# Small loads of the beginning on other queues, x in quarters, the first weights split by inner tiles, bias DMAs ahead of the first projection job

## The reference

```python
h = rms_norm(x, norm1_g[l])                                   # x: (1, 256, 1024)
p = jnp.einsum('bsd,de->bse', h, w_in[l])                     # w_in: (1024, 2560)
q, k, v = ...                                                 # 8 heads of 64 each
q = rms_norm(q, q_norm_g[l]); k = rms_norm(k, k_norm_g[l])
bias = rel_bias[:, jnp.clip(dist, -128, 128) + 128]           # (8 heads, 257) spread over distances
p = jax.nn.softmax(jnp.where(valid, q @ k.T * d ** -0.5 + bias, NEG_INF))
```

## Time and profile before

| | us |
|---|---|
| median of three runs | 1808.47 (1807.52 to 1809.2) |
| the profiled execution | 1807.76 |
| its span on the core | 1806.0 |
| PE busy | 1740.0 (96%) |
| DVE busy | 1336.2 (74%) |
| ACT busy | 1161.0 (64%) |
| POOL busy | 63.8 (4%) |

### The profile page before, as it was taken

One profiled execution on the slowest core, in us unless ns is written; L12 is line 12 of the kernel. 1 busy time (PEld: TensorE's weight loads), 2 busy tenths in 40 slices (PEclk: granted clock), 3 DMA queues, 4 the chain that ended last, 5 costly groups with the idle time before them and its releaser, 6 DMA issues.

```text
span 1806.0 us, 23347 instructions
## 1 busy us (share of the span) xinstructions
PE 1740.0 (96%) x8588; PEld 1427.8 (79%) x8588; DVE 1336.2 (74%) x1191; ACT 1161.0 (64%) x1179; POOL 63.8 (4%) x64
## 2 busy tenths in 40 slices
PE   7899999989999989889999999999999999999998
PEld 6677888877788876668888888888888888888886
DVE  5664444676554458568888898898888898888988
ACT  5545543665544358647777777777777776776775
POOL 1010000130000000020000000000000000000000
PEclk9899999999999999979999999999999999999999
DMA  9545553545556454139999989999999999999995
GB/s 340 168 151 177 186 187 123 175 154 163 189 184 192 158 174 129 39 124 360 374 326 371 366 326 365 349 346 367 344 353 370 329 370 364 325 366 348 345 368 224
DMA packets 230600, 481.74 MB, mean 267 GB/s; under 512 B 12020, under 2 KB 55560, under 8 KB 230544
## 3 DMA queue, kind: packets, MB, share of 16 engines
q1 hardware_dynamic: 220224, 470.99, 73.3%
q10 hardware_dynamic: 10320, 9.99, 1.7%
HBM read 479.08 MB, written 2.65 MB: 267 GB/s over the span
## 4 chain that ended last, share of the span: by engine, by line
PE 68%; DVE 5%; ACT 4%; issue 2%; ACTq 0%; DMA 0%; DVEq 0%; POOL 0%
PE bank L631 21%; PE bank L634 20%; PE bank L632 20%; PE bank L1179 2%; ACT w_hi L1744 1%; PE bank L1211 1%; PE bank L1066 1%; DVE x L2286 1%; DVE w_lo L2306 1%; PE bank L625 1%; DVE w_lo L1801 1%; ACT w_hi L1281 1%; ACT L1744 0%; ACT e L1363 0%; ACT dwq L1656 0%
## 5 line engine op out<-in xcount | busy, mean ns | idle before, releaser
L2306 DVE TENSOR_TENSOR w_lo<-raw,w_hi 128x2048 fp32r<-128x2048 f32 x336 | 764.3, 2289 | 118.5 <-ACT w_hi L1744 115.7
L1744 ACT ACTIVATE w_hi<-raw 128x2048 fp32r<-128x2048 f32 x336 | 639.3, 1920 | 173.3 <-PE bank L634 173.2
L1801 DVE TENSOR_TENSOR w_lo<-raw,w_hi 128x2048 fp32r<-128x2048 f32 (+3 forms) x118 | 256.0, 2173 | 150.9 <-ACT w_hi L1281 150.5
L631 PE MATMUL bank<-w_hi,xg_hi 128*128 128x512 f32 x896 | 355.7, 397 | 5.9 <-DVE w_lo L2306 4.4
L634 PE MATMUL bank<-w_hi,xg_lo 128*128 128x512 f32 x896 | 350.5, 391 | 0.0
L632 PE MATMUL bank<-w_lo,xg_hi 128*128 128x512 f32 x896 | 349.9, 391 | 0.0
L631 PE MATMUL bank<-w_hi,a_hi 128*128 128x512 f32 (+3 forms) x672 | 263.1, 391 | 12.5 <-DVE a_lo L2165 4.4
L1281 ACT ACTIVATE w_hi<-raw 128x2048 fp32r<-128x2048 f32 (+3 forms) x118 | 213.1, 1811 | 91.9 <-PE bank L634 85.5
L634 PE MATMUL bank<-w_hi,a_lo 128*128 128x512 f32 (+3 forms) x672 | 256.1, 381 | 0.0
L632 PE MATMUL bank<-w_lo,a_hi 128*128 128x512 f32 (+3 forms) x672 | 256.0, 381 | 0.0
L631 PEld LDWEIGHTS bank<-w_hi,xg_hi 128*128 128x128 f32 x896 | 169.0, 189 | 42.4 <-DVE w_lo L2306 7.3
(11 more groups left out here) (229 smaller groups left out, 1695.3 us busy)
## 6 DMA issues: line engine op xcount, KB each, us to landing
raw<-in_moe_w_gate SPq DMA_DIRECT2D x114, 1024.0 KB, 7.0
raw<-in_moe_w_up SPq DMA_DIRECT2D x113, 1024.0 KB, 7.1
raw<-in_moe_w_down SPq DMA_DIRECT2D x112, 1024.0 KB, 6.5
raw<-in_w_mlp SPq DMA_DIRECT2D x32, 1024.0 KB, 5.2
raw<-in_ffn_w_gate SPq DMA_DIRECT2D x22, 512.0 KB, 3.8
raw<-in_ffn_w_up SPq DMA_DIRECT2D x22, 512.0 KB, 4.8
raw<-in_ffn_w_down SPq DMA_DIRECT2D x11, 1024.0 KB, 4.8
raw<-in_w_in SPq DMA_DIRECT2D x10, 1024.0 KB, 12.2
```

The source lines that it names most:

```text
L631: pe.matmul(o, hi, h, start=start, stop=False)
L1744: act.activation(w_hi[:, g % NSPLIT, :], raw_at(g, GRAN), ACT.Copy).then_inc(hi_made, 1)
L1801: dve.tensor_tensor(w_lo[:, g % NSPLIT, 0:n], raw_at(g, n), w_hi[:, g % NSPLIT, 0:n].bitcast(F32), ALU.subtract).then_inc(lo_made, 1)
L2306: dve.tensor_tensor(w_lo[:, g % NSPLIT, :], raw_at(g, GRAN), w_hi[:, g % NSPLIT, :].bitcast(F32), ALU.subtract).then_inc(lo_made, 1)
```

## The change

- SP's list begins with the first quarter of x (256 columns), then `ident`, `gcol`, the first quarter of granule 0 (one inner tile), the second quarter of x, quarters 1 to 3 of granule 0, the rest of x. `masks`, `negtri` and `iota` go into SP's list ahead of the granules 7, 8 and 9.
- ACT's list begins with the issues of `rel_row` and of the two halves of `hcol`, and an activation on a column of its own (`warm_up`). Granule 0 is split in four quarters on ACT and DVE (`first_part`), between the transposed steps 0 and 1 and behind step 1; steps 2 and 3 of `norm1` are made by PE at the tiles 2 and 3 of `in0(0)`, and their copies stand behind the quarters on ACT and DVE.
- DVE extends `rel_row` behind the last quarter; ACT writes it out there, issues the band behind the split of granule 2, and `relT` behind the split of granule 5, ahead of the copy of job 1.
- The loads of `LOADS["early"]` and `pool_w` are issued by GpSimd, behind its `norm(NORM1)` and ahead of the roots of K.

```diff
+            load_x(0)
             sp.dma_start(ident[:], a["c_ident"]).then_inc(start_in, 16)
             sp.dma_start(gcol[:], a["g_norms"]).then_inc(start_in, 16)
-            for h in range(2):
-                sp.dma_start(x[:, :, h * 512:(h + 1) * 512], tokens(a["x"][0])[:, :, h * 512:(h + 1) * 512])\
-                    .then_inc(x_in[h], 16)
+            load_first(0)
+            load_x(1)
+            for kk in range(1, 4):
+                load_first(kk)
+            load_x(2)
+            load_x(3)
             for g, (parts, kts, n) in enumerate(stream):
+                if g == 0:
+                    continue
+                if g == NRAW:
+                    sp.wait_ge(first_lo, 3)
+                if NRAW < g <= NRAW + len(LOADS["const"]):
+                    dst, table = LOADS["const"][g - NRAW - 1]
+                    sp.dma_start(dst, table).then_inc(const_in[g - NRAW - 1], 16)
                 if g >= NRAW:
                     sp.wait_ge(lo_made, g - NRAW + 1)
...
             norm(NORM1)
+            for dst, src in LOADS["early"]:
+                pool.dma_start(dst, src).then_inc(early_in, 16)
+            pool.wait_ge(pool_zero, 1)
+            for gr in range(4):
+                r = (gr % 2) * HD
+                pool.dma_start(pool_w[r:r + HD, gr // 2, r:r + HD], a["pool_w"][0, gr]).then_inc(early_in, 16)
             heads_norm(N0K)
             heads_norm(N0Q)
...
             pe.wait_ge(start_in, 32)
-            for half in range(2):
-                norm_t("norm1", half, x, x_in[half], 16)
+            def first_t(s):
+                pe.wait_ge(x_in[s], 16)
+                tstep(at["norm1"]["t"] + s, [x[:, b, kt * P:(kt + 1) * P] for kt in (2 * s, 2 * s + 1) for b in range(NB)])
+            first_t(0)
+            first_t(1)
...
+            def first(kk):
+                if kk >= 2:
+                    first_t(kk)
+                if kk % 2 == 0:
+                    pe.wait_ge(t_dve, dve_steps(at["norm1"]["t"] + kk // 2))
+                if kk < 3:
+                    pe.wait_ge(first_lo, kk + 1)
+                else:
+                    pe.wait_ge(lo_made, 1)
-            in0(0)
+            in0(0, first)
...
+            act.dma_start(rel_row[:, 127:127 + 257], a["rel_bias"]).then_inc(rel_in, 16)
+            for dst, src in LOADS["gains"]:
+                act.dma_start(dst, src).then_inc(gains_in, 16)
+            act.wait_ge(eps_set, 1)
+            act.activation(warm_up[:], eps[:], ACT.Copy)
             act.wait_ge(start_in, 32)
-            for dst, src in LOADS["const"]:
-                act.dma_start(dst, src).then_inc(const_in, 16)
-            norm_hi("norm1", NORM1, 0)
-            hi_to(0)
+            t_hi(at["norm1"]["t"], a_at(a_hi, "norm1", 0, 2), gains(NORM1, 0))
+            first_part(0)
+            t_hi(at["norm1"]["t"] + 1, a_at(a_hi, "norm1", 2, 2), gains(NORM1, 1))
+            for kk in range(1, 4):
+                first_part(kk)
+            act.wait_ge(rel_ext, 1)
+            act.dma_start(rel_rows_dram, rel_row[:]).then_inc(rel_out, 16)
+            done[0] = 1
             norm_hi("norm1", NORM1, 1)
             hi_to(2)
+            act.wait_ge(rel_out, 16)
+            act.dma_start(rel_band_dram, ...).then_inc(rel_band, 16)
             squares(NORM1, x, scratch)
-            act.dma_start(rel_row[:, 127:127 + 257], a["rel_bias"]).then_inc(rel_in, 16)
-            for dst, src in LOADS["early"]:
-                act.dma_start(dst, src).then_inc(early_in, 16)
...
             square_heads(proj0, 512, REL_HEADS, j)
-            act.wait_ge(rel_ext, 1)
-            act.dma_start(rel_rows_dram, rel_row[:]).then_inc(rel_out, 16)
             hi_to(g + 4)
             hi_to(g + 5)
-            act.wait_ge(rel_out, 16)
-            act.dma_start(rel_band_dram, ...).then_inc(rel_band, 16)
+            act.wait_ge(rel_band, 16)
+            act.dma_start(relT[:], rel_band_dram.rearrange("h p m -> p h m")).then_inc(rel_back, 16)
             out_in0(1)
             square_heads(proj0, 0, REL_HEADS, j + 1)
             for k in range(2):
                 t_copy(at["k0"]["t"] + k, kT[:, 2 * k:2 * k + 2, :], GQ0 + 1)
             hi_to(g + 6)
-            act.wait_ge(rel_band, 16)
-            act.dma_start(relT[:], rel_band_dram.rearrange("h p m -> p h m")).then_inc(rel_back, 16)
...
+            t_lo(at["norm1"]["t"], a_at(a_lo, "norm1", 0, 2), a_at(a_hi, "norm1", 0, 2), gains(NORM1, 0))
+            first_part(0)
+            t_lo(at["norm1"]["t"] + 1, a_at(a_lo, "norm1", 2, 2), a_at(a_hi, "norm1", 2, 2), gains(NORM1, 1))
+            for kk in range(1, 4):
+                first_part(kk)
+            dve.wait_ge(rel_in, 16)
+            dve.tensor_copy(rel_row[:, 0:127], bcast(rel_row[:, 127], 127))
+            dve.tensor_copy(rel_row[:, 384:], bcast(rel_row[:, 383], REL_LEN + 1 - 384)).then_inc(rel_ext, 1)
+            done[0] = 1
             norm_lo("norm1", NORM1, 1)
             lo_to(2)
```

More of the change, by code:

```diff
@@ L242, in block_kernel @@
         eps = sb("eps", [P, 1])
-        sb("pad1", [P, 104])
+        warm_up = sb("warm_up", [P, 1])
+        sb("pad1", [P, 103])
         mixers = ExitStack()
@@ L408, in block_kernel @@
         LOADS = dict(
-            const=[(hcol[0:HD, :], a["g_heads"]),
-                   (hcol[HD:P, :], a["g_heads"]), (negtri[:], a["c_negtri"]), (iota[:], a["c_iota"]),
-                   (masks[:], a["c_masks"][:, :, 0, 0:P])],
+            gains=[(hcol[0:HD, :], a["g_heads"]), (hcol[HD:P, :], a["g_heads"])],
+            const=[(masks[:], a["c_masks"][:, :, 0, 0:P]), (negtri[:], a["c_negtri"]), (iota[:], a["c_iota"])],
             early=[(invcnt[:], a["c_invcnt"]), (cw[:], a["conv_w"]), (pscale[:], a["pool_scale"])],
@@ L586, in _ @@
             pool.wait_ge(dec_in, 32)
-            pool.wait_ge(const_in, 16 * len(LOADS["const"]))
+            for landed in const_in:
+                pool.wait_ge(landed, 16)
             for k in range(FOX_HEADS // 2):
@@ L690, in job_half @@
                     copied(before[-1])
-                pe.wait_ge(lo_made, g + half + 1)
+                if g + half > 0:
+                    pe.wait_ge(lo_made, g + half + 1)
                 across(g + half, n, a_tile(name), 4 * half, outs, half == 0, half == 1, middle)
@@ L1408, in t_copy, with first_part @@
                     act.activation(dst, src, ACT.Copy, scale=hcol[:, gain:gain + 1]).then_inc(t_act, 1)
-            act.wait_ge(start_in, 32)
-            for dst, src in LOADS["const"]:
-                act.dma_start(dst, src).then_inc(const_in, 16)
-            norm_hi("norm1", NORM1, 0)
-            hi_to(0)
+            act.dma_start(rel_row[:, 127:127 + 257], a["rel_bias"]).then_inc(rel_in, 16)
[3 more added lines that the diff above has]
+            act.activation(warm_up[:], eps[:], ACT.Copy)
+            act.wait_ge(start_in, 32)
+            def first_part(kk):
+                act.wait_ge(first_in[kk], 16)
+                cols = slice(kk * 512, (kk + 1) * 512)
+                ins = act.activation(w_hi[:, 0, cols], raw[:, 0, cols], ACT.Copy)
+                ins.then_inc(first_hi if kk < 3 else hi_made, 1)
+            t_hi(at["norm1"]["t"], a_at(a_hi, "norm1", 0, 2), gains(NORM1, 0))
[6 more added lines that the diff above has]
+            done[0] = 1
             norm_hi("norm1", NORM1, 1)
             hi_to(2)
+            act.wait_ge(rel_out, 16)
+            act.dma_start(rel_band_dram, bass.AP(rel_rows_dram.tensor, P - 1, [[REL_LEN + 1, REL_HEADS], [-1, P], [1, 384]]))\
+                .then_inc(rel_band, 16)
             squares(NORM1, x, scratch)
-            act.dma_start(rel_row[:, 127:127 + 257], a["rel_bias"]).then_inc(rel_in, 16)
-            for dst, src in LOADS["early"]:
-                act.dma_start(dst, src).then_inc(early_in, 16)
-            act.wait_ge(pool_zero, 1)
-            for gr in range(4):
-                r = (gr % 2) * HD
-                act.dma_start(pool_w[r:r + HD, gr // 2, r:r + HD], a["pool_w"][0, gr]).then_inc(early_in, 16)
             act.wait_ge(rstd_made, 1)
@@ L1956, in _ @@
             out_in0(0)
-            dve.wait_ge(rel_in, 16)
-            dve.tensor_copy(rel_row[:, 0:127], bcast(rel_row[:, 127], 127))
-            dve.tensor_copy(rel_row[:, 384:], bcast(rel_row[:, 383], REL_LEN + 1 - 384)).then_inc(rel_ext, 1)
             sum_heads(N0K)
@@ L1966, in _ @@
             lo_to(g + 6)
+            dve.wait_ge(const_in[0], 16)
             dve.wait_ge(rel_back, 16)
```

39 lines of the change are left out of this document (26 added, 13 removed).

## The result

The changed kernel takes **1826.17 us** (median of 4 runs, 1823.91 to 1830.0) where the kernel before, run beside it, takes 1808.84: a ratio of 1.0099 with an interval of [1.0087, 1.0111]. It is slower by some 17 us, where 8 were to be gained. Its profiled execution took 1827.54 us, with a span of 1825.7.

The account below looks back on a forecast made before the run. PE was taken as the bound, its opening held up by the bias chain: relT at 50 plus 13.6 put scores of pair 2 at 63.6, not 71.5; 7.9 us gained, 1799.9 or 1800.6 us; range 1795.3 to 1805.5.

Parts of the forecast that it names:

- The step that failed: Behind the first block: work is PE-bound with weights loaded ahead, so the opening's 7.9 us gain reaches the end unchanged.
- a late band: Bias chain, rival: the band waits in the full queue to near 49 or later; at 54, 1813 us; chance 0.05.
- relT's load: Bias chain: sharing all engines with granules 10 and 11, it takes 7 to 11 us, 9 taken, landing at 50.
- From relT to the scores of pair 2: First block: 15.0 us before, less 1.4 for the slow spell, so 13.6, giving scores of pair 2 at 63.6.
- The base: Opening: the old start of the scores of pair 2, 71.53 us, from which the gain was counted.
- The first projection matmul: Start of the opening: comes at 7.4 us instead of 14.08.
- the new wait for w_lo: Opening, behind granule 0: PE waits 3.7 us for DVE's split of granule 1, to near 20.4, with a clock fall.
- the band's copy: Bias chain: 1024 packets at 53 per us from 22, beside the weights, ending at 41.
- the stall ahead of kT: Ahead of the first block: ACT's wait for the band delays its copies to 44, stalling PE 1.3 us.
- seven GpSimd issues: Small loads behind rstd, ahead of the roots of K: 1 us each taken, nothing on the path.
- PE waits for relT anyway: First block: PE waits for relT, so the start's gain or loss (a loss of 0.65 us taken) disappears.
- Rival 1: Bias chain: band ends by 38, relT lands by 46 to 47, gain 10.9 to 1797.6 us; chance 0.25.

Follow-up runs that it names:

- twelve: Nine with the bias rows written twice, so that the band's copy has an outermost dimension of 16 instead of 8: 1796.75 us, ratio 0.993.
- Ten: The changed kernel on the old addresses, the band's copy given a second dimension (two halves behind the outer 8): 1805.12 us, ratio 0.998.
- seven: The kernel before with pad1 32 columns smaller, its rear tiles moved down by 128 bytes: 1829.71 us, ratio 1.0114.
- one: The aligned kernel: the changed kernel with pad1 cut from 103 to 96 columns, putting tiles at their old addresses: 1803.66 us, ratio 0.9975.
- nine: The changed kernel on the old addresses, granule 1 split ahead of the second half of norm1's copies: 1804.55 us, ratio 0.9975.
- eleven: The changed kernel on the old addresses with the edits of both nine and ten: 1804.55 us, ratio 0.9977.
- six: The kernel before with pad1 64 columns smaller, its rear tiles moved down by 256 bytes: 1809.01 us, ratio 1.0002.
- eight: The changed kernel on the old addresses, its three bias DMAs back at their old places in ScalarE's list: 1808.98 us, ratio 1.0006.

## Why the prediction was wrong, step by step

**The step that failed** is the one that carried the opening's gain to the end: "Everything behind the first block is PE-bound with its weights loaded ahead, so a shift of the opening should reach the end unchanged." It took for granted that the work behind goes at its old pace. It does not: three quarters of the wide matmuls (4776 of 6360) took 5 to 6 ns more, 22.5 us in all, and turned a gain of 5 into a loss of 17. The prediction's own last sign of being wrong is what came: the gain at the scores of pair 2 was not found again at the end of the span. The diff had the reason why it does not, in two lines that the prediction never priced: `warm_up` appeared in it as time on ACT alone, not as a tile that moves others. No rival held it, and the chance of 0.05 for slower stood on another mechanism, a late band, which did not happen. With the addresses put back the step itself holds: the aligned kernel is 3.1 us ahead at the scores of pair 2 and 2.8 at the end of the span, and twelve is 12.6 ahead at the one and 10.4 at the other. Ten's trace is the odd one: 2.6 ahead at the scores of pair 2 and 2.3 behind at the end. That execution took 1810.15 us, 5 more than the median of ten's runs, with a clock of 0.85 from 120 to 140 us. The spells at the lower clock fall differently from trace to trace: PE stands still for 2.7 us once between 122 and 142 us in all fourteen traces, and the clock fell to 0.50 at its end, for 3.4 or 6.8 us, in four of them (the changed kernel, seven, ten and twelve). So the prediction's reading, that idle times of 2.18 and 5.11 us make it fall, names an occasion and not a certainty.

**The size of the gain** was off too, for a kernel without the move: 1803.66 to 1805.12 us in one, nine, ten and eleven, a gain of 3.5 to 5.5, where 7.9 were forecast. The terms in the changed kernel, by its own rows (PE; ACT and its queue; DVE; POOL):

```profile
4.79 1.12 PE L654 MATMUL bank<-ident,x 128*128 128x128 f32 x4 [4.79 <-DMA gcol<-in_g_norms]
...
20.38 0.47 PE L660 MATMUL bank<-w_hi,a_hi 128*128 128x512 f32 x1 [3.75 <-DVE w_lo L1856]
...
42.48 1.14 PE L654 MATMUL bank<-ident,proj 128*128 128x128 f32 x8 [1.23 <-ACT kT L1455]
46.31 0.93 PE L778 MATMUL bank<-kT,qT 64*128 64x128 f32 x8
55.32 1.01 PE L778 MATMUL bank<-kT,qT 64*128 64x128 f32 x8 [2.42 <-DVE e L1966]
59.69 1.54 PE L793 MATMUL bank<-ident,e 128*128 128x128 f32 x6 [3.36 <-DVE e L1981]
67.48 0.93 PE L778 MATMUL bank<-kT,qT 64*128 64x128 f32 x8
```

```profile
39.53 0.40 ACTq L1500 DMA_DIRECT2D relT<-rel_band_dram  x1
39.98 0.69 ACT L1396 ACTIVATE proj<-bank,rstd 128x512 f32<-128x512 f32 x1 [6.44 <-DMA rel_band_dram<-rel_rows_dram]
```

```profile
52.61 1.23 DVE L2038 TENSOR_TENSOR relT<-relT,masks 128x1024 f32<-128x1024 f32 x1 [5.57 <-DMA relT<-rel_band_dram]
```

```profile
25.07 2.08 POOL L601 DMA_DIRECT2D pool_w<-in_pool_w  x4
...
31.46 2.94 POOL L565 TENSOR_TENSOR hroot<-hsum,mhalf 128x16 f32<-128x16 f32 x1
```

- **relT's load**, put at 9 us, took 13.0 (39.53 to 52.5; 12.6 to 13.1 in all kernels that issue it early, 6.9 and 7.0 in before and in eight). While it ran, SyncE's queue of weights had 65.6% of the engines' time, against 22.3% in the kernel before. Its issue was 1.5 us earlier than forecast, so relT was used at 52.61 and not at 50. This is 2.6 of the 3.9 us missing at the scores of pair 2.
- **From relT to the scores of pair 2** it was to be 13.6 us, without the slow spell, and was 14.9: the wait for the probabilities was 3.36 us and not 1.6, and the clock fell again (0.80 over 50 to 60 us, 0.86 over 60 to 70). The other 1.3 us. The sum had missed that scores of pair 1 wait for DVE's adds of pair 0 (2.42), because DVE makes these adds only from 53.88 on, behind relT, and without Q's wait PE is there by 52.9.
- **The base**: 71.53 was an early draw. Two other kernels with the old bias chain, six and eight, had their scores of pair 2 at 73.71 and 74.64 and the time of before. Against these the aligned kernel's 68.40 is 5.3 to 6.2 earlier, near the 5.5 us by which its median is lower.
- **The first projection matmul**, forecast for 7.4, was at 8.51. gcol, now behind a quarter of x, held PE to 4.79 and not 3.9. It cost nothing at the end.

**What held:** the new wait for w_lo, 3.75 us to 20.38 (forecast 3.7 to 20.4), though without the fall of the clock there (its mean is 1.00 to 50 us; in one, eight and ten, with the same wait, it is 0.93, 0.93 and 0.97); the band's copy, 1031 packets at 53 per us from 20 on (forecast 53 from 22), over at 39 and not 41; the stall ahead of kT, 1.23 us (1.3); seven GpSimd issues of 0.5 to 0.8 us each (1 taken), over at 27.2, ahead of K's roots at 31.46; and "PE waits for relT anyway", which kernel eight shows for the start (no gain alone) and twelve for relT (used 7.5 us earlier, with the scores of pair 2 8.5 us earlier). Rival 1, where the band gets through early, is what twelve made true: it forecast relT by 46 to 47, the scores of pair 2 at 60.6 and 1797.6 us, and they came at 45.08, 58.97 and 1796.75.

## To carry to other kernels

Read a diff for the tiles that it adds, and compare the addresses of all tiles before and after: here a tile of 4 bytes stood at 137312 and the next at 137344, which put the operands of 4776 of the 6360 wide matmuls 32 bytes further apart and cost 22.5 us. When a kernel grows slower and no wait has grown, look at the mean of its largest group of matmuls and at its count in a fixed stretch, and repeat the change on the old addresses before any other explanation. For a small table that is spread by a copy on a critical chain, look at the outermost dimension first: going from 8 to 16 (50 packets per us, then 95) was worth 7.8 us here, more than all the rest of the change with its 3.5 to 5.5.

## What the runs showed of the hardware

- A matmul of 512 columns, back to back, takes 226.5 to 228.9 ns here (means of groups, float32r operands) when the distance from its moving to its stationary operand within a partition is a multiple of 256 bytes (70656, 95232 and the like), and 231.7 to 235.0 when it is 32, 64 or 128 off. Nine kernels have the one distance and five the other for xg, mf, f and m, and in all of them a_hi and a_lo, whose distance never changed, kept 227.3 to 228.5. On this kernel it is 1.1 to 1.3% of the time. Where in TensorE it arises no run shows.
- A copy from DRAM to DRAM of 1.5 MB ran at 48 to 53 packets per us (20 to 28 us) with an outermost dimension of 8 and at 95 with 16. The weight queue beside it had 77 to 84% of the engines' time with 8, and 58.6% with 16.
- The same load of relT took 6.9 us when the weight stream was thin (22.3% of the engines' time) and 12.6 to 13.1 when it was full (65.6%).
- The same idle time of 2.7 us of TensorE, at the same place of the program, came with a granted clock of 0.50 at its end, for 3.4 or 6.8 us, in four of fourteen traces, and not in the other ten.
- The granted clock is 0.50 or 1.00 in every record of the fourteen traces. At 0.50 matmuls of 512 columns started 0.427 us apart (in the kernel before, at 66.06 and 66.48, with the clock at 0.50 from 63.85 to 67.26), which is 1.2 columns per ns: the prediction's 1.2 GHz is this pace.
